# Attention over key and value pages beside a state-space scan: when the pages are used among the projection tiles and heads

## The reference

```python
z = h @ P['od_w_in'][o]                       # 1024 -> 2048: q, k, v, u
q, k = rmsnorm(q, ...), rmsnorm(k, ...)       # per head of 64
k_all = concatenate([k_past, k]); v_all = concatenate([v_past, v])   # past: 1024 rows in pages of 128
# every query scores each past block of 256 rows by q . mean(k of the block), keeps the best 3 and its own,
# softmax over q . k + bias in the kept ones, times v
o_c = moba_attend(q, k_all, v_all, pos0, P['rel_bias'])
y, hr, hi = s5_scan(u, s_re, s_im, ...)       # h_t = A h_{t-1} + B u_t,  y_t = Re(C h_t) + D u_t
o_d = glu(gelu(y))
out = concatenate([o_c, o_d]) @ P['od_w_out'][o]
```

## Time and profile before

| | |
|---|---|
| median of 3 runs | 1145.46 us |
| profiled execution: its time | 1150.5 us |
| profiled execution: span of its instructions | 1148.7 us |
| PE busy | 1067.2 us (93%) |
| DVE busy | 655.6 us (57%) |
| ACT busy | 388.5 us (34%) |
| DMA, mean | 167 GB/s |

### The profile page before, as it was taken

The page is one execution under the profiler, slowest core; times in us unless marked ns, Lnnn a source line. Parts: engine busy times, 40 slices in busy tenths (PEclk is TensorE's granted clock), DMA queues, the critical chain, the costliest instruction groups (busy, mean ns, idle before and its releaser), DMA issues.

```text
span 1148.7 us, 20544 instructions
## 1 busy us (share of the span) xinstructions
PE 1067.2 (93%) x8206; PEld 902.2 (79%) x8206; DVE 655.6 (57%) x1420; ACT 388.5 (34%) x729; POOL 100.1 (9%) x202
## 2 busy tenths in 40 slices
PE   7998999978998999999999988788999989999996
PEld 5877977856885899999988543444788769999996
DVE  6865553143314588886746447664341458998642
ACT  3523222422134444444412002421312454444330
POOL 0010021211000012221000000000100001222100
PEclk9988978968999999999999988799999999999998
DMA  8421115316446255565453887168754635555540
GB/s 323 144 79 39 40 42 184 110 43 256 134 141 238 88 182 180 182 211 207 144 198 111 295 259 240 38 220 254 311 178 143 224 127 177 182 181 195 208 152 38
DMA packets 41568, 192.40 MB, mean 167 GB/s; under 512 B 4602, under 2 KB 5754, under 8 KB 24578
## 3 DMA queue, kind: packets, MB, share of 16 engines
q1 hardware_dynamic: 36146, 167.37, 42.2%
q0 software_dynamic: 4288, 22.15, 5.1%
q10 hardware_dynamic: 1040, 1.57, 0.4%
HBM read 183.72 MB, written 7.35 MB: 166 GB/s over the span
## 4 chain that ended last, share of the span: by engine, by line
PE 74%; issue 9%; SPq 5%; DVE 5%; DMA 3%; ACT 3%; POOL 1%; DVEq 0%; ACTq 0%; POOLq 0%
PE bank L1238 73%; SPq L639 3%; SPq L625 3%; ACT work L793 1%; DVE work L1876 1%; DMA ring<-in_ck 1%; DVE work L1873 1%; DMA ring<-in_pool_k 1%; PE bank L1241 1%; ACT work_r L793 1%; DMA x<-in_x 1%; DMA ring<-in_pool_v 0%; DVE smx L1957 0%; DVE tmp L1873 0%; DVE oT L1873 0%
## 5 line engine op out<-in xcount | busy, mean ns | idle before, releaser
L1238 PE MATMUL bank<-h,ring 128*128 128x264 f32 x896 | 215.2, 399 | 0.0
L1238 PEld LDWEIGHTS bank<-h,ring 128*128 128x128 f32 x896 | 175.5, 197 | 35.3 <-issue 4.0
L1238 PE MATMUL bank<-h_r,work_r 128*128 128x264 f32 x704 | 200.6, 285 | 0.0
L1238 PE MATMUL bank<-h_r,ring_r 128*128 128x264 f32 x704 | 200.2, 284 | 0.0
L1238 PE MATMUL bank<-sq_r,work_r 128*128 128x264 f32 x704 | 199.9, 284 | 0.0
L793 ACT ACTIVATE work_r<-ring 128x2048 fp32r<-128x2048 f32 (+1 forms) x60 | 125.1, 2089 | 191.0 <-PE bank L1238 191.0
L1873 DVE TENSOR_TENSOR ring_r<-ring,work_r 128x2048 fp32r<-128x2048 f32 (+1 forms) x60 | 150.2, 2506 | 46.9 <-ACT work_r L793 46.8
L1238 PEld LDWEIGHTS bank<-sq_r,work_r 128*128 128x128 f32 x704 | 132.5, 188 | 0.1
L1238 PE MATMUL bank<-work_r 128*128 128x264 f32 x704 | 129.7, 285 | 3.0 <-DVE ring_r L1873 2.9
L1238 PEld LDWEIGHTS bank<-h_r,ring_r 128*128 128x128 f32 x704 | 132.4, 188 | 0.0
L1238 PEld LDWEIGHTS bank<-h_r,work_r 128*128 128x128 f32 x704 | 132.2, 188 | 0.1
(11 more groups left out here) (251 smaller groups left out, 1131.8 us busy)
## 6 DMA issues: line engine op xcount, KB each, us to landing
ring<-in_gu SPq DMA_DIRECT2D x44, 1024.0 KB, 4.9
ring<-in_down SPq DMA_DIRECT2D x16, 1408.0 KB, 6.1
ring<-in_pool_k SPq DMA_DIRECT2D x64, 256.0 KB, 3.6
ring<-in_pool_v SPq DMA_DIRECT2D x64, 256.0 KB, 3.3
ring<-in_ev_in_a SPq DMA_DIRECT2D x8, 1024.0 KB, 6.7
ring<-in_ev_in_b SPq DMA_DIRECT2D x8, 1024.0 KB, 4.9
work<-in_cv POOLq DMA_DIRECT2D x8, 1024.0 KB, 11.9
ring<-in_ck SPq DMA_DIRECT2D x8, 1024.0 KB, 4.9
```

The lines of the kernel that those rows point to most:

```text
L1238: return nc.tensor.matmul(out, lhsT, rhs, start=start, stop=stop, skip_group_check=True)
```

## The change

Five things, all in the odd mixer.

1. P0 to P4 stand behind t8, t10, t12, t14 and t15, P5 to P7 in heads 0 to 2. SP's program stays the same, instruction for instruction.
2. `choose_pages` compares all pairs of the four blocks by six comparisons and adds up by one reduction, where 20 small operations, each waited for, stood.
3. `s5_output_matrices` runs on DVE between tiles 12 and 14, where it stood in heads 0 and 1. For that its results and the samples' old states (`s5h`) lie in the ring's last columns, which page and projection slots leave free, and no longer in `h`; POOL loads `s5h` early, without a wait for t15, and reaches the stores of the new keys and values (`o_k`, `o_v`) that are behind it in its program without that wait.
4. In the heads everything stands a step or more earlier: `s5_matrices` and their copies in step 3 (was 4), the last score rows and `choose_pages` in 3 (was 4), `page_weights` in 4 (was 5), `pt` in 5 (was 7), `sample_inputs` in 1 (was 5), `sample_states` in 2 (was 5).
5. V0, V1 and V2 stand in steps 6, 7 and 8; the loop behind the heads starts with V3 before x_1 and ends with three rounds without a V.

The diff, cut:

```diff
+KEYS_AT = (8, 10, 12, 14, 15)
...
-        if m >= 9 and m % 2:
-            key_pages((m - 9) // 2)
+        if m in KEYS_AT:
+            key_pages(KEYS_AT.index(m))
...
-        if i < 4:
-            key_pages(4 + i)
-        if i == 4:
+        if i < 3:
+            key_pages(5 + i)
+        if i == 3:
             order.extend([("s5ab", 0), ("s5ab", 1), ("s5k",)])
+        if i == 1:
+            order.extend([("s5s", j) for j in range(4)])
         if i == 5:
-            order.extend([("s5s", j) for j in range(4)])
-        if i == 7:
             order.extend([("pt", "moba", j) for j in range(4)])
+        if i in (6, 7, 8):
+            value_pages(i - 6)
         if i == 8:
             order.extend([("s5x", 0), ("s5x", 1)])
+
+    def value_pages(i):
+        for m in (2 * i, 2 * i + 1):
+            stream("pv", m, 2048, ("so", "moba", m // 4) if m % 4 == 3 else None)
+        if i % 2:
+            order.append(("so", "moba", i // 2))
...
+    for i in range(NT // 2):
+        if i + 3 < NT // 2:
+            value_pages(i + 3)
+        if i + 1 < NT // 2:
+            order.extend([("s5x", 2 * i + 2), ("s5x", 2 * i + 3)])
+        if i % 2 == 0 and i:
+            order.append(("s5y", i // 2 - 1))
...
-        s5cp = hf_[:, 0:1536].rearrange("p (q n k) -> p q n k", q=3, n=NT)
-        s5h = hf_[:, 1536:1792].rearrange("p (q n s) -> p q n s", q=2, n=NT)
+        s5cp = [ring[:, q, 2048:2560].rearrange("p (n k) -> p n k", n=NT) for q in range(3)]
+        s5h = ring[:, 3, 2048:2304].rearrange("p (q n s) -> p q n s", q=2, n=NT)
...
+            pool.dma_start(s5h, A["s5h"]).then_inc(s5h_in, 16)
...
-            full(pool, ("lin", "od_in", 15))
-            pool.dma_start(s5h, A["s5h"]).then_inc(s5h_in, 16)
...
+            for i in range(NT // 2):
+                if i in (0, 2, 4):
+                    samples_out(osm, i // 2 + 1)
+                if i + 1 < NT // 2:
+                    inputs_out(i + 1)
...
-            cnt = gsm[:, 2, :].rearrange("p (g b) -> p g b", g=2)
-            cmp_ = gs2[:, 0, :]
+            beats = tmpf[:, 436:460].rearrange("p (g b n) -> p g b n", g=2, b=4)
 
             def choose_pages():
 
-                for b in range(4):
-                    first = True
-                    for b2 in range(4):
-                        if b2 == b:
-                            continue
-                        op = ALU.is_ge if b2 < b else ALU.is_gt
-                        if first:
-                            step(tt(cnt[:, :, b], gv[:, :, b2], gv[:, :, b], op))
-                        else:
-                            step(tt(cmp_, gv[:, :, b2], gv[:, :, b], op))
-                            step(tt(cnt[:, :, b], cnt[:, :, b], cmp_, ALU.add))
-                        first = False
+                for d in range(1, 4):
+                    low, high = gv[:, :, 0:4 - d], gv[:, :, d:4]
+                    tt(beats[:, :, d:4, 3 - d], low, high, ALU.is_ge)
+                    ins = tt(beats[:, :, 0:4 - d, d - 1], high, low, ALU.is_gt)
+                step(ins)
+                step(V.tensor_reduce(gsm[:, 2, :], beats.rearrange("p g b n -> p (g b) n"), AX, ALU.add))
...
                     own_score()
-                    s5_output_matrices(0)
                 if i == 1:
-                    s5_output_matrices(1)
+                    score_rows(2)
                 if i == 2:
-                    score_rows(2)
-                if i == 4:
+                    sample_states()
+                if i == 3:
                     score_rows(3)
                     choose_pages()
-                if i == 5:
-                    sample_states()
+            score_rows(0)
             od_in(12)
-            score_rows(0)
+            s5_output_matrices(0)
             od_in(13)
+            s5_output_matrices(1)
             od_in(14)
+            score_rows(1)
             od_in(15)
-            score_rows(1)
             dve.wait_ge(bias_in, 16)
```

More of the change, by code:

```diff
@@ L124, in lin @@
                 slots.append(("w", name, m // per_slot, cols, None))
-            slot_of[(name, m)] = len(slots) - 1
+            slot_of[(name, m)] = slot_of[(name, m - 1)] if m % per_slot else len(slots) - 1
             order.append(("lin", name, m))
-            slots[-1] = slots[-1][:4] + (("lin", name, m),)
+            at = slot_of[(name, m)]
+            slots[at] = slots[at][:4] + (("lin", name, m),)
             if after:
@@ L865, in copy_out, with samples_out @@
                 drain(f(dst, src, ACT.Copy), key)
[L867 to L877, removed]
+            def samples_out(dst, i):
+                key = ("so", "moba", i)
+                full(act, key)
+                for s_ in (2 * i, 2 * i + 1):
+                    r = 32 * (s_ % 4)
+                    ins = f(dst[r:r + H, s_ // 4, :], bank(key)[r:r + H, :], ACT.Copy)
+                drain(ins, key)
             def attend(name, n, hd, after=None):
@@ L1756, in pages @@
                     end(ins)
[L1757 to L1759 removed]
+                if i < 3:
+                    key_pages(5 + i)
+                if i == 3:
                     s5_matrices()
+                if i == 1:
+                    sample_inputs()
                 if i == 5:
[L1762 to L1763 removed]
                     for k in range(4):
@@ L1794, in y_pair @@
                     for n in tiles:
-                        mm(o(n, LS, L), s5cp[:, w, n, :], p(n, f_, q), w == 0, w == 2 and q == 1)
+                        mm(o(n, LS, L), s5cp[w][:, n, :], p(n, f_, q), w == 0, w == 2 and q == 1)
                 for n in tiles:
@@ L1813, in x_pair, with value_pages @@
                                 close(ins, ("s5x", n))
-            attend("moba", H, 64, zo[:, 0:4, :], zo[:, 4:8, :], ovt, pages)
-            for i in range(4):
-                drained(pe, ("pt", "moba", i))
-            for n in range(0, NT, 2):
+            def value_pages(i):
+                if i == 0:
+                    for j in range(4):
+                        drained(pe, ("pt", "moba", j))
+                n = 2 * i
                 key = ("so", "moba", n // 4)
@@ L1830, in _ @@
                             slot_done(ins, "pv", n + m)
-                if n + 2 < NT:
-                    x_pair(n // 2 + 1)
-                if n:
-                    y_pair(n // 2 - 1)
+            attend("moba", H, 64, zo[:, 0:4, :], zo[:, 4:8, :], ovt, pages)
+            for i in range(NT // 2):
+                if i + 3 < NT // 2:
+                    value_pages(i + 3)
+                if i + 1 < NT // 2:
+                    x_pair(i + 1)
+                if i:
+                    y_pair(i - 1)
             y_pair(NT // 2 - 1)
```

46 lines of the change are left out of this document (14 added, 32 removed).

## The result

| | before | after |
|---|---|---|
| median, runs of one chip | 1147.28 us (1144.44 to 1149.4, 4 runs) | 1185.92 us (1183.92 to 1188.33, 4 runs) |
| ratio, 95% interval | | 1.0339 [1.0303, 1.0375] |
| profiled execution, its span | 1150.5, 1148.7 us | 1184.55, 1182.8 us |

The changed kernel is slower by 38.6 us where the prediction had 29.3. 1185.92 lies 11 us above the predicted 1174.8, at the upper end of the range (1186).

A forecast was written before the change was run, and what follows sets the result against it. SP's own issuing was taken to bound both page stages, at 8.6 us a pair. The terms 25.9 - 12.9 + 0 + 16.3 = +29.3 us on 1145.46 gave 1174.8 us, range 1162 to 1186.

The forecast's parts named there:

- The rival that the pages come in time: Key pages among the tiles: SP alone sets the pace, -5.7 us in place of +25.9, 1143.2 us in all; chance 0.08.
- Part 1: Key pages among the tiles, up to P7's end: +25.9 us, bounds +15.8 to some +33.
- P1's landing: Landing of the last page DMA ahead of P1: 5.35 us, between a quiet 3.94 and a crowded 6.75.
- The chain at the further pairs: Each pair after P1: second tile 3.65, refill chain 10.35 and pair 6.5, 20.5 us where it was 10.87.
- t15 to P7's end: Last key pages, bound by SP's issuing: t15 ends at 699.6 us and P7 at 735.0.
- I take 6.5: P1, P2 and P3 each start at the low clock after their waits and take 6.5 us, 3.6 kept for the range.
- the clock stays up: Rival for P1 to P3: PE recovers its clock before it counts; -8.7 us, 1166.1 us in all; chance 0.20.
- more low clock: Rival: P4 to P7, the heads and the rounds behind V7 run low too; up to +15 us, 1184; chance 0.12.
- Part 2: Heads, from P7's end to V0: 22.9 us where it was 35.7, -12.9 us, between -8 and -14.
- Part 3: V0 to V7, at SP's pace: 0, from -2 to +3, around the 58.2 us of before.
- Part 4: Behind V7, up to y_7: 24.5 us against 8.2, +16.3 us, from +14 to +18.
- The matrices "cost nothing": Scan's matrices on DVE between the tiles: no cost, both under 19 us against 41 us from P1's end to P3's.

The follow-up runs named there:

- e1: Changed kernel with the key pairs put back behind the second tile of each weight slot; 1157.57 us, 1.0067 of the kernel before.
- e10: Changed kernel with SP loading the page numbers of both slots of a pair before waiting for the first slot; 1183.60 us, 1.0308 of the kernel before.
- e5: Changed kernel with POOL waiting for t15 again, so the stores of new keys and values leave after it; 1187.82 us, 1.0335 of the kernel before.
- e3: Changed kernel with V3 to V7 spread over rounds 0, 2, 4, 6 and 7 behind the heads; 1175.21 us, 1.0240 of the kernel before.
- e7: Changed kernel with score_rows(2) in DVE's step 0 in place of step 1; 1186.91 us, 1.0328 of the kernel before.
- e9: Changed kernel with filling matmuls on constants ahead of the waits of P1 to P4, by turns into two 32-row groups; 1181.95 us, 1.0292 of the kernel before.
- e11: Changed kernel with the scan's matrices back in DVE's steps 0 and 1 of the heads; 1187.94 us, 1.0356 of the kernel before.
- e8: Changed kernel with keys behind both tiles, score_rows(2) in step 0, value pairs behind x_i in rounds 0, 2, 4, 5, 6; 1140.10 us, 0.9925 of before.
- e6: Changed kernel with filling matmuls on constants ahead of the waits of P1 to P4, all into one 32-row group; 1201.39 us, 1.0456 of the kernel before.

## Where the prediction held, and which term was too small

**Direction and mechanism held.** The root was that a pair behind the first tile of a weight slot waits for pages that SP can only ask for after the second tile of the slot before, with one tile of work in between. P1, P2 and P3 wait 11.27, 8.69 and 6.43 us for in_pool_k, and e1, which changes nothing but that order, takes 31 us back. The rival that the pages come in time is refuted by these waits.

**Part 1 is the term that was mis-sized: +32.9 in place of +25.9.** By its steps:
- *P1's landing, "I take a landing of 5.35 us, the middle of 3.94 and 6.75": it was 9.02.* This is the step that failed most, 3.7 us. The 6.75 us were P1's own landing in the kernel before, with the bias table but without the stores; so the prediction took less than the same pair had needed, though it named the stores as coming on top, and it did not count their bytes. (That landing and PE's work behind it, 639.41 to 657.41, also lie on the chain of before, which from 633 us on is thus not nearly all SP's issuing.) From the first page DMA at 628.35 to P1 at 643.45 SP, ACT and POOL had asked for eight pages (2048 KB), the bias table (1536), the stores of the keys (528) and w6 (1024), 5136 KB or 5.26 MB; at the 393 GB/s of the fullest window that is an estimate of 13.4 us, where the sum had 4.29 + 1.64 + 5.35 = 11.3 from first DMA to landing and the trace has 15.0. Counted alike, e10 has the same 13.4 by bytes and 14.3 in the trace, though its DMAs were issued 2.2 us faster, and without the stores e5 and the kernel before have 12.0 by bytes and 13.2 and 12.7 in their traces. So the landing follows the bytes; the 0.7 to 1.6 us on top stay unexplained.
- *The chain at the further pairs.* P2 starts 22.4 us behind P1 where 20.5 were expected: SP stood 1.7 us longer between the two slots (8.11 us for the eight DMAs, 6.40 ahead of P1), in a load of a page number that took 1.83 us where others take 0.27. This too goes with the early stores: the load stands 1.3 us behind POOL's store of the new values (654.34), it takes 1.81 to 1.86 us in e3, e7, e9 and e11, and 0.27 in e5, where a load of 1.67 us stands behind the moved stores instead. By what way a store holds up the load stays open; behind those of e1 (636.69 and 639.44) no load took over 0.34 us. P3 follows in 19.2 us, since P2 was a little less slow (5.42) and the landing 3.84. Chain of waits, that load in the changed kernel and, second, in e5:

```profile
655.67 1.83 SPq L635
...
658.73 0.27 SPq L635
```

- *t15 to P7's end, 38.3 us where 35.4 were expected.* The prediction had SP's pages alone; in the trace P4 takes 6.53 us and P6 waits for its bank. e7 took the bank's wait away and met SP's pages: 32.6 us from t15's end to P7 (736.14 less 703.53) where the chain had 31.8, and then P7 at 5.21 us for its low clock. So it is 0.8 us of pages and 1.6 of clock, or the bank in their place.
- *The clock.* "I take 6.5" for three pairs: they took 6.36, 5.42 and 6.07, and e9 shows that this is low clock behind a wait and not the pair's work. The rival "the clock stays up" falls with the same rows; "more low clock", which gave 1184, is nearest in time, but by luck: P4 (6.53 us) and P6 (5.22) were as slow before (6.48, and P6 from 696.38 to 702.93), and the larger part of the miss is P1's landing. The Trainium skill ("TensorE: Matmul & The Clock Gate", HAM oscillation) says that a loop which waits for DMAs before each short burst starts every burst at the low clock; by P1 to P4 (6.36, 5.42, 6.07 and 6.53 us) the trace agrees.

The Trainium skill's figure for a DMA ("DMA: Bandwidth & Descriptors", Anatomy of one DMA), by which a 256 KB page was estimated at 2.6 us, is fitted there to single DMAs that GpSimd issues, while SP issues the pages here. It would have made part 1 smaller still; the landings were 3.84 to 9.02 us, and the measurement decides.

**Part 2: -9.7 in place of -12.9, between the bounds given.** "The samples' states on DVE now lie in step 2, where PE waits for P7's pages": PE did not wait for P7 (729.53, no wait), because P6's bank had already held it. DVE's timeline of the changed kernel, the first and last of the states and the scores of head 3 behind them:

```profile
732.94 0.62 DVE L1889 TENSOR_TENSOR oT<-ring,s5par 128x128 f32<-128x128 f32 x2
...
737.51 0.36 DVE L2533 COPY oT<-s5o 128x128 f32<-128x128 f32 x2
737.79 0.68 DVE L1892 SCALAR_TENSOR_TENSOR work<-bank,work 128x512 f32<-128x512 f32 x1
```

P7 ended at 733.16, so these scores were due 2.7 us later at 735.9 and came at 737.79: 1.9 us of states on the path. The rest is low clock in one step: PT and O of a head, priced at 1.8 us from no row, took 3.4 (747.85 to the drain that ends at 751.25), at a granted clock of 0.57 from 740 to 752 us; the other steps together took 0.3 us less than their prices. In e7 and e8, where DVE is done with its score rows earlier, the stage is 24.6 and 24.7 us.

**Part 3: 0, as predicted**; V0 to V7 is 58.2 us in both. **Part 4: +16.4 against +16.3**: x_5 to x_7 behind V7 make DVE's rounds the path. (The prices listed for it add up to 25.0 us and not to 24.5, with 0.6 for each of the two output steps; measured were 24.7.) DVE's timeline of the changed kernel, the rounds of x_5 and x_7 (their first operations, as in the earlier trace rows) and the last products:

```profile
823.62 3.10 DVE L1889 TENSOR_TENSOR work<-work 128x512 f32<-128x512 f32 x5 [4.26 <-ACT work L802]
...
832.96 3.07 DVE L1889 TENSOR_TENSOR work<-work 128x512 f32<-128x512 f32 x5
...
837.86 1.29 DVE L1889 TENSOR_TENSOR work<-work 128x512 f32<-128x512 f32 x2
```

e3, which spreads the value pairs over the rounds, takes 16.5 us off this stage and gives 7.3 back between V0 and V7; its time is 11 us less.

**The matrices "cost nothing" between the tiles**: held, and by e11 they would have cost next to nothing in the heads too, so in this order this part of the change neither gave nor took.

## What to carry to other kernels

When a change moves a consumer closer to the release of its buffer, compare the whole refill chain (release, issue, landing) with the work left in between; where it is longer, every round pays the difference and then the low clock behind it. In a stage that waits for transfers, price the landing by all the bytes due in that stretch against the best rate that a window shows, not by the middle of two landings. Taking one transfer out of that stretch only moved the wait here (e5); issuing faster helped, though the landings took back part of it (e10). Where two waits end together, taking one away gives nothing (e7). Keep the engine with the longest serial round fed ahead of the work that can wait (e8).

## What the runs showed of the hardware

The same matmul of 128x512 with 32 rows of output costs half when two groups of 32 rows take turns: 44 records (two to a matmul) in 9.63 us (0.22 each) in e9, 43 in 18.64 us (0.43) in e6. It was no low clock: the window of e6 inside that filling (columns as in the earlier trace rows) has a granted clock of 1.00, where after has 0.55 in the same window.

```profile
640.00:650.00 10.00, 10.00 (x25) 2.53 (x23) 0.00 (x0) 0.00 (x0) 0.00 (x0) 1.00 0.74 288
```

The Trainium skill ("TensorE: Matmul & The Clock Gate", Part 3: Packing small matmuls) says that outputs in different groups of 32 rows fall on different column groups of the array and run at once. The two runs agree, by a factor of 2 for two groups.

A landing was longer when its DMAs were issued closer together: the last of the same eight pages landed in 10.46 us when they were issued in 4.19 us (e10), and in 9.02 when they were issued in 6.40 (8.87 to 9.78 in e3, e7, e9 and e11). The stores beside a pair were worth 2.0 us of landing at P1 and 2.8 at P4 (e5).

A load of a page number by SP mostly took 0.27 us, but some loads behind a 528 KB store of POOL took far longer: 1.83 us, 1.3 us behind the store of the new values in the changed kernel, 1.56 at 670.71 behind that at 669.48 in the kernel before, and 1.67 behind the moved stores in e5. It isn't so behind every store (at most 0.34 us in e1).
